# A two-layer attention, Hyena and mixture-of-experts step on one core: weight ring, routing and share sums rebuilt

## The reference, cut to what matters

```python
def adaln(cvec, w, b):                     # w is 1024 x 6144
    m = jax.nn.silu(cvec) @ w + b
    return [t[:, None, :] for t in jnp.split(m, 6, axis=-1)]

# layer: sh1, sc1, g1, sh2, sc2, g2 = adaln(...)
h = rmsnorm(x, norm_mix[l]) * (1 + sc1) + sh1
x = x + g1 * mixer(h)                      # ends in a 1024x1024 output product
h = rmsnorm(x, norm_ffn[l]) * (1 + sc2) + sh2
x = x + g2 * hier_moe(h)

def hier_moe(h, ...):                      # top-1 of 4 groups, top-2 of its 8 experts
    ids = g_i * EXPERTS_PER_GROUP + e_i
    gates = jnp.sum(one_hot(ids, 32) * weights[..., None], axis=1)
    hg = jnp.einsum('nd,edf->nef', t, w_gate)    # 32 experts of 1024 x 256
    hu = jnp.einsum('nd,edf->nef', t, w_up)
    return jnp.einsum('nef,efd->nd', silu(hg) * hu * gates[:, :, None], w_down)
```

## Time and profile before

| | us |
|---|---|
| median of 3 runs | 1317.21 |
| lowest, highest | 1314.58, 1325.98 |
| profiled execution, its time | 1313.93 |
| its span, first to last instruction | 1312.2 |
| TensorE busy | 1158.4 (88%) |
| VectorE busy | 582.9 (44%) |
| mean granted TensorE clock | 0.924 |

### The profile page before, as it was taken

How to read it: one execution, slowest core, us unless ns; L and a number is a source line. 1 busy time by engine, 2 the same in 40 slices (tenths; PEclk the granted TensorE clock), 3 DMA queues, 4 the chain that set the end, 5 groups by cost and what they waited for, 6 DMA issues and landing times.

```text
span 1312.2 us, 26081 instructions
## 1 busy us (share of the span) xinstructions
PE 1158.4 (88%) x9139; PEld 678.4 (52%) x9140; DVE 582.9 (44%) x1209; ACT 265.3 (20%) x644; POOL 210.9 (16%) x257
## 2 busy tenths in 40 slices
PE   3799867989955899999979999999986699999996
PEld 3554445755454455555555654344545455555553
DVE  0123342453342444444454334677644344444445
ACT  1111232432101111211132212222011111212111
POOL 1024220000111222222200001111010122222221
PEclk9699977999958999999989999899995799999998
DMA  9624139996284999999942313000038499986893
GB/s 316 227 78 175 65 139 351 328 372 230 79 363 183 418 392 395 417 410 377 396 172 66 126 37 125 0 0 1 0 106 373 186 404 421 413 372 254 322 423 160
DMA packets 83502, 317.34 MB, mean 242 GB/s; under 512 B 11160, under 2 KB 12097, under 8 KB 58089
## 3 DMA queue, kind: packets, MB, share of 16 engines
q1 hardware_dynamic: 78730, 304.95, 59.7%
q0 software_dynamic: 1952, 6.90, 1.3%
q10 hardware_dynamic: 2752, 4.53, 0.9%
HBM read 307.82 MB, written 8.54 MB: 241 GB/s over the span
## 4 chain that ended last, share of the span: by engine, by line
PE 81%; DMA 6%; DVE 5%; issue 2%; SPq 2%; POOL 1%; ACT 1%; POOLq 0%; DVEq 0%
PE banks L431 78%; DMA arena<-in_ada_b 3%; DVE arena L952 3%; DMA arena<-slot_rows 2%; SPq L1827 1%; PE banks L598 1%; POOL slot_rows L1731 1%; DMA mod_rows<-arena 1%; DMA slot_rows<-arena 1%; SPq L1825 1%; PE banks L482 1%; PE banks L793 0%; DVE arena L998 0%; POOL arena L1720 0%; PE banks L546 0%
## 5 line engine op out<-in xcount | busy, mean ns | idle before, releaser
L431 PE MATMUL banks<-arena 128*32 128x128 f32 (+9 forms) x8712 | 1101.5, 420 | 90.0 <-DMA arena<-in_ada_b 17.4
L431 PEld LDWEIGHTS banks<-arena 128*32 128x32 f32 (+4 forms) x8712 | 623.1, 155 | 541.4 <-issue 386.7
L952 DVE TENSOR_TENSOR arena<-banks,arena 128x64 f32<-128x64 f32 (+4 forms) x284 | 114.0, 413 | 111.6 <-PE banks L431 77.1
L952 DVE TENSOR_TENSOR arena<-arena 128x384 f32<-128x384 f32 (+11 forms) x229 | 153.8, 677 | 4.4
L1207 DVE SCALAR_TENSOR_TENSOR arena<-arena 128x768 f32<-128x768 f32 x81 | 83.2, 1027 | 92.1 <-issue 87.9
L1748 POOL COPY arena<-arena 128x256 f32 x79 | 66.2, 838 | 186.3 <-PE banks L431 147.0
L1581 ACT ACTIVATE arena<-banks 128x512 f32<-128x512 f32 x79 | 47.2, 597 | 241.2 <-PE banks L431 241.2
L1739 POOL TENSOR_TENSOR arena<-arena 128x256 f32<-128x256 f32 x81 | 59.4, 733 | 219.2 <-PE banks L431 219.2
L1217 DVE TENSOR_SCALAR arena<-arena 128x64 f32<-128x64 f32 x79 | 15.4, 195 | 167.5 <-ACT arena L1585 167.5
L1719 POOL TENSOR_SCALAR arena<-arena 128x8 f32<-128x8 f32 (+2 forms) x28 | 10.4, 372 | 384.2 <-ACT arena L1440 266.5
L1306 DVE TENSOR_SCALAR arena<-arena 128x385 f32<-128x385 f32 x24 | 11.6, 482 | 82.4 <-ACT arena L1642 82.4
(11 more groups left out here) (144 smaller groups left out, 460.0 us busy)
## 6 DMA issues: line engine op xcount, KB each, us to landing
arena<-in_moe_w_gate SPq DMA_DIRECT2D x64, 1024.0 KB, 8.2
arena<-in_moe_w_up SPq DMA_DIRECT2D x64, 1024.0 KB, 10.5
arena<-in_moe_w_down SPq DMA_DIRECT2D x64, 1024.0 KB, 10.5
arena<-in_ada_w SPq DMA_DIRECT2D x24, 2048.0 KB
arena<-in_hy_w_in SPq DMA_DIRECT2D x6, 2048.0 KB
arena<-in_attn_w_in SPq DMA_DIRECT2D x3, 2048.0 KB
arena<-slot_rows SPq DMA_DIRECT2D x6, 1024.0 KB, 7.3
arena<-mod_rows SPq DMA_DIRECT2D x8, 512.0 KB, 9.6
```

The source lines that it names most:

```text
L431: return pe.matmul(out, lhsT, rhs, start=start, stop=stop, skip_group_check=True)
L952: return dve.tensor_tensor(o, p, q, op)
```

## The change

Four things change.

1. **Ring and order of the ada chunks.** "up" keeps its place to the end of the units, while six chunks pass through the two others; seven chunks are worked off in units 6 to 12 and thirteen in the pairs, before two and eighteen. The units are issued two ahead, with banks named by hand. The bias load and the POOL work on it move ahead.
2. **Output product by token tile**, with the residual and the norm behind it; the first two tiles are transposed ahead of the logits.
3. **Routing.** The slot of each token comes from one PSUM sum (`rank` with the prefix added in it). DVE makes one-hot rows of it (`lanes`, `tiles`), and six products (`inv`) give the token of each slot. The token rows are stored to `token_rows` in their own order by ACT, and POOL gathers them straight into SBUF, one semaphore for each of six gathers.
4. **Share sums.** The same twelve products, eight in the first group and four in the second, over other banks.

```diff
+        def place_of(n):
+            return n % 3 if n < 9 else (n - 9) % 2 if n < 15 else (n + 2) % 3
-        at_unit = {7: chunks[0], 9: chunks[1]}
-        at_pair = {int(1.32 * n) + 1: c for n, c in enumerate(chunks[2:])}
+        at_unit = {6 + n: c for n, c in enumerate(chunks[:7])}
+        at_pair = {int(1.9 * n) + 1: c for n, c in enumerate(chunks[7:])}
...
-                w = item(arrived((kind, i // 3)), KC, 512)
-                t = i % 3
+                w = item(arrived((kind, i % 2)), KC, 512)
+                t = i // 2
...
                 for n, (kind, t) in enumerate(units):
-                    if n + 1 < len(units):
-                        if units[n + 1] == ("q", 0):
+                    if n + 2 < len(units):
+                        if units[n + 2] == ("q", 0):
...
-                        produce(*units[n + 1])
+                        produce(*units[n + 2])
                     if n in at_unit:
-                        ada(*at_unit[n])
+                        ada(*at_unit[n], 7)
                     turn_unit(kind, t)
...
+                transposes(u, (0, 1))
+                logits(0)
+                logits(1)
+                transposes(u, (2,))
+                close(logits(2), "logit", l)
...
+                for t in (2, 1, 0):
+                    for s in range(t + 1):
+                        mm(o[:, t * NE:(t + 1) * NE], upper if s == t else ones, both[:, s, :], s == 0, False)
+                    sig("count").at(pe, l)
+                    last = mm(o[:, t * NE:(t + 1) * NE], cc[0:NE, 0:P], upE, False, True)
+                close(last, "rank", l)
...
+                sig("lo").at(pe, l)
+                o = open_(pe, "inv", l, [("slots", l)])
+                for c in range(6):
+                    last = mm(o[:, 0:ST], lanes[:, c, :], tiles[:, c, :], c == 0, c == 5)
+                close(last, "inv", l)
...
-                    pe.wait_ge(rows_back[i // 2], 16 * (l + 1))
+                    pe.wait_ge(rows_gathered[i], 16 * (l + 1))
...
-                            q = 2 * hf + (t + half) % 2
...
+                    two = ((2, 0), (2, 2), (0, 1), (0, 3), (0, 0), (0, 2), (1, 1), (1, 3))
+                    share_parts(two, shares, rows_, start).then_inc(s_["moe_half"], 1)
...
+                    return share_parts(((1, 0), (1, 2), (2, 1), (2, 3)), shares, rows_, start).then_inc(s_["moe_shared"], 1)
...
+                link(tt(twice, oh12, bc(slot_of, 2, 1), ALU.mult))
+                link(dve.tensor_reduce(pos[:, 0:6], twice.rearrange("p q (t e) -> p (q t) e", t=T), AX, ALU.add))
+                link(dve.tensor_copy(slot_i, pos[:, 0:6]))
+                link(dve.tensor_scalar(tile_i, slot_i, int(math.log2(P)), None, ALU.logical_shift_right))
+                link(dve.tensor_scalar(tile_base, tile_i, float(P), None, ALU.mult))
+                link(tt(lane_of, pos[:, 0:6], tile_base, ALU.subtract))
+                link(tt(tiles, bc(tile_base, ST, 2), bc(tile_starts, 6, 1), ALU.is_equal))
+                tt(tiles, tiles, bc(token_ids, ST, 2), ALU.mult)
+                for c in range(6):
+                    ins = dve.tensor_scalar(lanes[:, c, :], lane, lane_of[:, c:c + 1], None, ALU.is_equal)
...
+                    act.dma_start(tokens_d[u // 2][t * P:(t + 1) * P, :], h[:, t].rearrange("p k q -> p (k q)")).then_inc(rows_stored, 16)
...
+                pool.wait_ge(rows_stored, 16 * T * (l + 1))
                 sig("slots").at(pool, l)
-                for r in range(2):
-                    for t in range(T):
-                        c = r * T + t
-                        to = bass.IndirectOffsetOnAxis(ap=slot_of_token[:, c:c + 1], axis=0)
-                        pool.indirect_dma_start(slots_d[l], to, h[:, t].rearrange("p k q -> p (k q)"), None).then_inc(rows_scattered, 16)
+                for i in range(ST):
+                    of = bass.IndirectOffsetOnAxis(ap=token_of_slot[:, i:i + 1], axis=0)
+                    pool.indirect_dma_start(slot_rows[:, i, :], None, tokens_d[l], of).then_inc(rows_gathered[i], 16)
...
-                sp.wait_ge(rows_scattered, 16 * 2 * T * (l + 1))
-                for i in range(ST // 2):
-                    src = slots_d[l][i * 2 * P:(i + 1) * 2 * P].rearrange("(o p) n -> p o n", p=P)
-                    sp.dma_start(slot_rows[:, 2 * i:2 * i + 2, :], src).then_inc(rows_back[i], 16)
```

More of the change, by code:

```diff
@@ L192, in in_turn @@
                 o += n
-        in_turn("routed", [(n, 1) for n in ("logit", "gx", "choice", "count", "pref", "slots", "pos")])
-        in_turn("psum_routed", [(f"psum_{n}", 1) for n in ("logit", "rank", "count", "pref")])
+        in_turn("routed", [(n, 1) for n in ("logit", "gx", "choice", "count", "steps", "lo", "pref", "slots", "pos")])
+        in_turn("psum_routed", [(f"psum_{n}", 1) for n in ("logit", "count", "rank", "pref", "inv")])
+        in_turn("loop_ends", [("zeroed", 1), ("share_last", 1)])
+        in_turn("act_moe", [("gexp", 1), ("moe_end", 1)])
+        in_turn("psum_latents", [("psum_qlat", 1), ("psum_kvr", 1)])
+        in_turn("set_up", [("cT", 1), ("gains", 1)], False)
+        in_turn("act_latents", [("nv", 3), ("latT", 4)], False)
         in_turn("hyena_once", [("col", 1), ("net", 2), ("ncol", 4)], False)
@@ L293, in build @@
         for n, k in enumerate(items):
-            loads[n % 3] += 16 * ndma.get(k[0], 1)
-            landed[k] = loads[n % 3]
+            loads[place_of(n)] += 16 * ndma.get(k[0], 1)
+            landed[k] = loads[place_of(n)]
         item_loaded = [sem(f"item_loaded{i}") for i in range(3)]
@@ L309, in build @@
         out_sem = sem("outputs_stored")
[L310 to L311 removed]
+        rows_stored = sem("rows_stored")
+        rows_gathered = [sem(f"rows_gathered{i}") for i in range(ST)]
         n_out = [0]
@@ L371, in build @@
         rw = v(WORK + 6832, 768)
-        slot_of_token = v(WORK + 6832 + 588, 6).bitcast(I32)
+        lane = v(WORK + 7600, P)
+        twice = v(WORK + 7728, 2, T * NE)
+        slot_i, tile_i, token_of_slot = (v(WORK + 7920 + 6 * i, 6).bitcast(I32) for i in range(3))
+        tile_base, lane_of = v(WORK + 7938, 6), v(WORK + 7944, 6)
+        tiles = v(WORK + 7950, 6, ST)
+        lanes = v(HTO + 1536, 6, P)
         xcur = v(WORK + 8368, KC, M)
@@ L633, in moe @@
                         last = mm(o_logit[:, t * 36:(t + 1) * 36], hT[:, k, t * P:(t + 1) * P], WR[:, k, :], k == 0, k == KC - 1)
-                close(last, "logit", l)
+                    return last
+                transposes(u, (0, 1))
[3 more added lines that the diff above has]
+                close(logits(2), "logit", l)
                 sig("choice").at(pe, l)
                 both = v(WORK + 6832 + 480, T, NE)
-                o = open_(pe, "rank", l, [("pos", l)])
-                for t in range(T):
-                    for s in range(t + 1):
-                        last = mm(o[:, t * NE:(t + 1) * NE], upper if s == t else ones, both[:, s, :], s == 0, s == t)
-                close(last, "rank", l)
-                o = open_(pe, "count", l, [("count", l)])
+                o = open_(pe, "count", l, [("steps", l)])
                 for t in range(T):
@@ L646, in moe @@
                 close(last, "count", l)
-                sig("count").at(pe, l)
+                o = open_(pe, "rank", l, [("pos", l)])
+                for t in (2, 1, 0):
[4 more added lines that the diff above has]
+                close(last, "rank", l)
+                sig("steps").at(pe, l)
                 o = open_(pe, "pref", l, [("pref", l)])
@@ L1036, in attention @@
                     sig("hms").by(red, n)
+                mean_squares(0)
+                for n, (kind, t) in enumerate(units):
+                    if n + 1 < len(units):
+                        mean_squares(n + 1)
+                    if n - 1 in at_unit:
+                        ada_row(at_unit[n - 1])
+                    b = n % 2
                     sig("hrs").at(dve, n)
@@ L1819, in load @@
                 n = number[k]
-                if n >= 3:
-                    wait_used(sp, items[n - 3])
-                s = item_loaded[n % 3]
+                held = [m for m in range(n) if place_of(m) == place_of(n)]
+                if held:
+                    wait_used(sp, items[held[-1]])
+                s = item_loaded[place_of(n)]
                 if k[0] == "ada":
```

165 lines of the change are left out of this document (83 added, 82 removed).

## The result

The changed kernel takes 1281.87 us, median of 4 (1279.75 to 1284.28), against 1321.6 for the kernel before in the same comparison: a ratio of 0.9747, 95% interval 0.9703 to 0.9791. (The two medians alone give 0.970.) It is faster by 2.5%, half of what was forecast. The profiled execution took 1279.75 us with a span of 1278.0, 34.2 less than that of before.

A forecast was written before the change was run, and what follows sets the result against it. TensorE was taken to bound both expert loops, with attention's pairs also held by late ada chunks and routing by waits. Sum: 1313.9 - 22 (attention) - 18 (routing) - 26 (loops) = 1248 us, range 1228 to 1282.

The forecast's parts named there:

- Loops, forecast -26: Both expert loops: regrouped share sums save 0.43 us a step, 34 us in all, of which 26 kept (-15 to -34).
- so what a group loses, the step loses: Expert step: TensorE is busy 5.89 of 5.91 us, so 0.43 us saved in the sums shortens each step by that.
- The deduction of 8 us for the weight stream: Expert loops: expert loads limit layer 0 to about 10 of its 16.3 us; with 16 in layer 1, 26 remain of 34.
- the first rival: Expert loops: weight loads bound them, so the share sums give nothing; total 1274 us, chance 0.14.
- Attention, forecast -22: Attention's units and pairs: pairs begin at 196 and end at 288.4 us instead of 310.2 (-12 to -31).
- the 15.8 us of the earlier trace: Units: TensorE's waits for VectorE, which issuing two units ahead was to hide; 9 us of waits were still assumed.
- The ring's 7.7 us of waits: Pairs: TensorE's waits for ada chunks, forecast to go because the first chunks are there when the pairs begin.
- the rival of SyncE and the ring: Attention: SyncE stands 8.8 us for the store's round trip with chunks late behind it, cancelling the gain; 1270 us, chance 0.13.
- Routing, forecast -18: Both routings: transposed tiles end sooner as gathers replace scatter and read back; -9 us a layer (each -5 to -13).
- The turns ahead: Routing: two tiles turned during TensorE's 2.88 us wait leave one of two gaps between the logits, -2.5 us.
- the rival of the clock: Routing: TensorE, working where it waited, runs at 2.4 GHz instead of 1.2, some 7 us a layer; 1233 us, chance 0.13.
- the slower rival: Expert loops: TensorE reaches experts before their weights and loses clock; 1353 us if 30 of 56 loads do, chance 0.03.

The follow-up runs named there:

- experiment 1: Changed kernel with the old division of the share sums (six products in each group) in the new banks: 1282.54 us, ratio 0.9759.
- experiment 2: Changed kernel with the groups of share sums exchanged, four products first and eight last: 1322.36 us, ratio 1.0047 to the kernel before.
- experiment 3: Changed kernel with TensorE's register reads for the next expert behind the first group of sums: 1284.61 us, ratio 0.9786.
- experiment 5: Changed kernel with TensorE's register reads for the next expert behind the hidden product of the step: 1267.19 us, ratio 0.9594.
- experiment 6: Changed kernel with 128 more instructions (semaphore increments nobody reads) executed by TensorE in the routing of layer 1: 1280.87 us, ratio 0.974.
- experiment 9: Changed kernel with register reads behind the hidden product and 128 skipped instructions in TensorE's routing of layer 1: 1257.0 us, ratio 0.9573.
- experiment 10: Changed kernel with register reads behind the hidden product and 192 skipped instructions in TensorE's routing of layer 1: 1262.08 us, ratio 0.9605.
- experiment 7: Changed kernel with the old ring and the old times of the adaLN chunks (two in the units, eighteen in the pairs): 1280.74 us, ratio 0.9733.
- experiment 11: Changed kernel with old ring, old adaLN chunk times and POOL's four bias operations again behind unit 5: 1277.38 us, ratio 0.9713.
- experiment 8: Changed kernel with the turns of each token tile again between the logits: 1288.03 us, ratio 0.9753.

## Why the prediction was wrong

The sign was right, the sum was twice too large, and the miss lies in one term.

**Loops, forecast -26, measured +3.3.** The step that failed is "so what a group loses, the step loses": 0.43 us at each of 79 steps. The group did lose it, full sets cost what half-full ones cost (1.06 to 0.71), and where a step stays with its expert it fell from 5.90 to 5.50. But only 15 of the 79 steps do. The 64 others end an expert, 48 of them inside a round, and before the next expert stands register work on TensorE's own sequencer. The earlier trace rows couldn't show it: that step stays with its expert, and one step was taken for all. Before, the work lay almost wholly under the last group (5.93 us for a step with it, 5.90 without). Its cover shrank with the group, so 5.93 became 5.86, not 5.50, and 6.47 at a round's change 6.38. By these prices the division was worth some 11 us (15 x 0.40 and 64 x 0.07 to 0.09), not 34. I asked what else was late on other engines and not on TensorE itself. Experiments 1 to 3 and 5 show it.

The rest went early in the loops. Layer 1's first eleven steps took 81.1 us where they had taken 71.5 (layer 0's 72.9 and 73.7), and the first steps began 1.9 and 1.4 us later in their windows than before; behind the eleventh step the two loops together became 9.0 us shorter. That the early stalls aren't of the division is shown (experiment 1). That the place of the code sets them is well supported, by one profile of each placing (experiments 6, 9, 10), and that each stall waits for its fetch is argued from the times.

The estimate from what the Trainium skill, "TensorE: Matmul & The Clock Gate", section "Why this matters for your kernels", gives for four small products side by side (3.07 times, measured there at 512 columns) would have made it 24 us instead of 34. The trace has full sets at no extra cost, and neither figure met the cause. The deduction of 8 us for the weight stream had no ground in the changed kernel: TensorE waits there for no expert in either loop, and at 5.50 a step the stream cost 3.4 us at the end of layer 0. So the first rival, that the weights bound the loops, gave a nearly right total (1274) for a wrong reason.

**Attention, forecast -22, measured -18.9.** The size was near, the reason was not. I let the units get 3.8 us later and the pairs 25.6 shorter, by chunks that came in time and by the clock. In experiments 7 and 11, without ring and chunks moved, the pairs end at 293.4 and 291.3, so all of it stays within the noise: what counted was the 15.8 us of the earlier trace rows, which I booked as 9 left, and of which 5.0 are left in experiment 7, with the units issued ahead and VectorE's order changed (which of the two is open). The ring's 7.7 us of waits didn't go; they are 12.1 in the changed kernel, moved in part to the units. So the mechanism of the rival of SyncE and the ring was there, chunks came late, but the gain that it was to cancel came from elsewhere and stayed; that the total came near is luck. (Thirteen chunks at 6.1 us each are 79 us, not the 76 of the sum; against the need of 90 it changes nothing.)

**Routing, forecast -18, measured -20.1.** Right by its steps. The turns ahead were costed at 2.5, and gave 2.6 and 3.1 (experiment 8). The first gather came 34.1 us behind the output product instead of 35.3 for the first scatter, so 1.2 sooner where I had 1.0. The last gather landed 6.31 us behind its issue, between the scatter's 4.29 and the 10.52 of the read back and nearer to the first, as taken. The mean clock hardly rose (0.66 and 0.64, from 0.62 and 0.61), so the rival of the clock fell.

No expert loop was starved, and the slower rival fell.

## What to carry to other kernels

Before a saving on the engine that bounds is booked, ask what its own sequencer does beside that work: here register reads and branches were covered by the last 12 to 15 matmul records in the queue, and their cover was how long these took (1.1 to 1.9 us), not how much work had been queued. Put such reads behind the longest instructions of the step. Price a step of each kind, not one step for all. And before a change of several parts is credited to one of them, undo them one by one: here the ring looked like the gain and gave none that can be told from noise.

## What was not expected of the hardware

- TensorE's sequencer ran only 12 to 15 matmul records ahead of fp32 products. 1.83 us of register work showed 0.29 us behind a mixed end of the queue and 0.8 behind eight products in full sets; 1.5 us of it showed 0.5 behind the first group and nothing behind the hidden product. The Trainium skill, "TensorE: Matmul & The Clock Gate", section "Architectural detail: the array is 16× 32×32, not 1× 128×128", gives this queue 64 entries. The trace has two matmul records for each fp32 product; how many entries of the queue it takes no run here shows.
- Code comes by DMA in packets of 16 KB. In the first passes of a loop TensorE stalled up to 2.7 us near them. With 128 instructions that are never run ahead of it, layer 1's loop took 234.3 us instead of 243.5, one profile of each.
- Four fp32 products with 32 rows each, side by side, took as long as two: the step is 5.90 us with half-full sets and 5.50 without.
